# Filter taps and filter spectra joined into one block, with the filter network's vectors loaded as columns

## What is computed

```python
mod = jax.nn.silu(c) @ ada_w[l] + ada_b[l]          # the same for c_ctx
h = jnp.sin(fr * (z @ w1 + b1))
h = jnp.sin(fr * (h @ w2 + b2))
h = jnp.sin(fr * (h @ w3 + b3)) @ w4                # the taps, (L, 1024)
h = h * jnp.concatenate([decay, decay], axis=-1)
k = jnp.concatenate([hf, zeros, hb[:0:-1]], axis=0)
k = k / jnp.sum(jnp.abs(k), axis=0, keepdims=True)
y = irfft(rfft(v) * rfft(k))                        # rfft(k) is what the spectra are for
```

## Time and profile before

| | |
|---|---|
| median of three runs | 1666.65 us (1663.92 to 1668.58) |
| the profiled execution, its time | 1668.4 us |
| its span in the trace | 1666.5 us |
| instructions | 22924 |
| busy share of the span: PE, DVE, ACT, POOL | 94%, 59%, 29%, 29% |
| first block ends, second starts | about 90 us |
| second block ends, third starts | about 136 us |

### The profile page before, as it was taken

How to read it: one execution, slowest core, us unless ns; L and a number is a source line. 1 busy time by engine, 2 the same in 40 slices (tenths; PEclk the granted TensorE clock), 3 DMA queues, 4 the chain that set the end, 5 groups by cost and what they waited for, 6 DMA issues and landing times.

```text
span 1666.5 us, 22924 instructions
## 1 busy us (share of the span) xinstructions
PE 1565.5 (94%) x9583; PEld 1438.0 (86%) x9583; DVE 991.2 (59%) x1370; ACT 491.2 (29%) x694; POOL 485.9 (29%) x218
## 2 busy tenths in 40 slices
PE   4797999999989979899999999999999999999996
PEld 1386789988989969799889999999999999999995
DVE  5547233776534336813788827864884687288845
ACT  1565122232243237543522211310320221122203
POOL 1557121323121139225422322321331322232210
PEclk9889999999989989999999999999999999999998
DMA  8563313344343687520011101101101101101102
GB/s 338 185 253 152 158 40 121 129 165 148 109 157 123 231 257 255 172 92 26 4 48 51 51 29 48 51 28 50 51 26 51 51 26 51 51 26 51 51 13 114
DMA packets 110569, 168.10 MB, mean 101 GB/s; under 512 B 5755, under 2 KB 87811, under 8 KB 105347
## 3 DMA queue, kind: packets, MB, share of 16 engines
q1 hardware_dynamic: 109039, 164.24, 28.4%
q10 hardware_dynamic: 1428, 2.40, 0.5%
HBM read 135.35 MB, written 31.27 MB: 100 GB/s over the span
## 4 chain that ended last, share of the span: by engine, by line
PE 55%; DVE 3%; ACT 1%; issue 0%; POOL 0%; ACTq 0%; DVEq 0%
PE psum L231 18%; PE psum L233 18%; PE psum L235 18%; DVE mlp_acc_a L3056 1%; DVE tail_scan_h L2936 1%; PE psum L3160 0%; PE psum L3320 0%; DVE mlp_h_lo L2942 0%; DVE w_raw L3125 0%; DVE mlp_h_lo L2930 0%; DVE mlp_acc_a L3125 0%; DVE tail_x L3080 0%; DVE mlp_h_lo L2987 0%; ACT tail_x L2833 0%; PE psum L3191 0%
## 5 line engine op out<-in xcount | busy, mean ns | idle before, releaser
L231 PE MATMUL psum<-mlp_h_hi,w_hi 128*128 128x384 f32 (+2 forms) x1248 | 304.5, 339 | 6.2 <-DVE mlp_acc_a L3056 3.5
L233 PE MATMUL psum<-mlp_h_lo,w_hi 128*128 128x384 f32 (+2 forms) x1248 | 301.0, 336 | 0.0
L235 PE MATMUL psum<-mlp_h_hi,w_lo 128*128 128x384 f32 (+2 forms) x1248 | 300.8, 336 | 0.0
L3056 DVE SCALAR_TENSOR_TENSOR w_raw<-psum,par,w_raw 128x945 f32<-128x945 f32 (+2 forms) x176 | 214.7, 1220 | 90.7 <-ACT w_raw L2877 87.0
L3056 DVE SCALAR_TENSOR_TENSOR mlp_acc_a<-psum,par,mlp_acc_a 128x945 f32<-128x945 f32 (+2 forms) x176 | 214.5, 1219 | 33.1 <-ACT mlp_acc_a L2877 29.9
L2648 POOL TENSOR_TENSOR w_lo<-w_raw,w_hi 128x2048 fp32r<-128x2048 f32 x32 | 148.1, 4628 | 288.4 <-ACT w_hi L2642 288.4
L231 PEld LDWEIGHTS psum<-mlp_h_hi,w_hi 128*128 128x128 f32 x1248 | 205.0, 189 | 25.4 <-issue 6.3
L233 PEld LDWEIGHTS psum<-mlp_h_lo,w_hi 128*128 128x128 f32 x1248 | 206.2, 189 | 15.2
L235 PEld LDWEIGHTS psum<-mlp_h_hi,w_lo 128*128 128x128 f32 x1248 | 206.0, 189 | 15.3
L3080 DVE SCALAR_TENSOR_TENSOR tail_x<-psum,mod,tail_x 128x384 f32<-128x384 f32 (+1 forms) x192 | 94.8, 515 | 128.3 <-PE psum L235 128.1
L233 PE MATMUL psum<-tail_g_lo,w_hi 128*128 128x384 f32 x480 | 160.3, 334 | 0.0
(11 more groups left out here) (372 smaller groups left out, 2524.3 us busy)
## 6 DMA issues: line engine op xcount, KB each, us to landing
w_raw<-ffn_w_up SPq DMA_DIRECT2D x22, 1024.0 KB, 5.0
filt_ada<-ada_w SPq DMA_DIRECT2D x16, 1024.0 KB, 8.6
w_raw<-w_in SPq DMA_DIRECT2D x13, 1024.0 KB, 5.5
w_raw<-ffn_w_down SPq DMA_DIRECT2D x11, 1024.0 KB, 5.0
scan_rows_spread<-scratch_scan_rows SPq DMA_DIRECT2D x18, 512.0 KB, 5.5
rownorm_ada<-ada_w SPq DMA_DIRECT2D x8, 1024.0 KB, 7.6
rownorm_x<-x_sample SPq DMA_DIRECT2D x8, 512.0 KB, 8.0
scratch_kt<-kt_spec SPq DMA_DIRECT2D x4, 1024.0 KB, 4.1
```

Source lines behind the costliest of these rows:

```text
L231: ins = nc.tensor.matmul(out, wh, x_hi(k, i), start=begin, stop=False)
L233: ins = nc.tensor.matmul(out, wh, x_lo(k, i), start=False, stop=False)
L235: ins = nc.tensor.matmul(out, wl, x_hi(k, i), start=False, stop=end)
L3056: ins = stt(out=out, in0=image(up_at)[:, r0 + dy:r1 + dy, c0 + dx:c1 + dx], scalar=weight(i, loc, t), in1=out, op0=ALU.mult, op1=ALU.add)
```

## The change

The two blocks become one, `filter_and_spectra`.

- The four vectors of the network come as columns (`vec`, eight DMAs of 64 elements each), no longer through `rows` and the transpose. PE's first two matmuls are those of the first layer.
- The first operation of the argument, bias and frequency, moves from DVE to ACT (`scale_product`, an Identity with a scale and a bias); DVE makes `shifts = bias * freq` once.
- SP loads the first layer's weights and the first part of `ada_w` ahead of the rest; `w4`, the rows and the cosine tables take other places in its list.
- The 16 parts are spread as 6 over the network's halves, 1 in each of the steps 1 to 6, 2 in step 7, and 2 behind the first group of the spectrum. The first group of the modulation is copied in step 3 and turned in step 4, the second after step 8.
- Groups 0, 1 and 2 of the spectrum stand before the closing sums of the taps; the prompt's spectrum comes after them. The PSUM banks of `pair(g)` are exchanged for that, and the squares, roots and scalings of the RMS norm move on by one group.
- The cosine tables are split in steps 4 and 5 instead of 6 and 7.

```diff
+def filter_and_spectra(nc, io, mem, dram, buffers, k_hi, k_lo, norm, stage, spec_out):
+    PARTS, RING = 2 * KD, FILTER_RING
+    TURN_AT = 4
     PIECE = FW // 2
+    STEPS4 = [(kt, half) for kt in range(2) for half in range(2)]
...
+        ring = WeightRing(nc, ph, mem, lambda u: (full, 1 + 6 * u if u else 4), ahead=2)
         ps, par = mem["psum"], mem["par"]
-        ADA_BANK = 6
...
-        conv += [(io["c"][0].rearrange("(b p) -> b p", p=P), 60, 8), (io["c_ctx"].rearrange("(b p) -> b p", p=P), 68, 8)]
...
-        filt = [(io[n], 76 + i) for i, n in enumerate(("hy_filt_b1", "hy_filt_b2", "hy_filt_b3", "hy_freq"))]
...
+        vectors = [io[n].rearrange("o p -> p o") for n in ("hy_filt_b1", "hy_filt_b2", "hy_filt_b3", "hy_freq")]
...
-        sizes = [2, 3, 3] + [1, 1, 2, 2, 2, 0, 0, 0] + [0]
+        sizes = [2, 2, 2] + [1, 1, 1, 1, 1, 1, 2, 2]
         part_at = [range(sum(sizes[:i]), sum(sizes[:i + 1])) for i in range(len(sizes))]
         assert sum(sizes) == PARTS
-        FORWARD_AT = (6, 7)
+        FORWARD_AT = (4, 5)
+        FORWARD_AFTER = 8
...
+        def pair(g):
+            first = (2, 0, 6, 4)[g % 4]
+            return ps[:, first:first + 2, :]
+        def sums_at(g):
+            return g + 1 if g < 3 else g + 2
...
-            sp.dma_start(mem["ident"][:], io["k_ident"]).then_inc(ident_in, 16)
+            def load_layer(src, i, n, sem):
+                for half in range(2):
+                    at_ = 64 * half
+                    sp.dma_start(wide[at_:at_ + n, i, at_:at_ + 64], src).then_inc(sem, 16)
             sp.dma_start(h[:], io["k_z"]).then_inc(mlp_in, 16)
             sp.wait_ge(wide_zero, 1)
-            for src, i, n in layer_w:
-                for half in range(2):
-                    at_ = 64 * half
-                    sp.dma_start(wide[at_:at_ + n, i, at_:at_ + 64], src).then_inc(mlp_in, 16)
+            load_layer(*layer_w[0], mlp_in)
...
                 if p == 0:
+                    sp.dma_start(mem["ident"][:], io["k_ident"]).then_inc(ident_in, 16)
+                    for layer in layer_w[1:]:
+                        load_layer(*layer, layers_in)
+                if p == 1:
                     for half in range(2):
                         sp.dma_start(w4[64 * half:64 * half + 64, :], io["hy_filt_w4"][0]).then_inc(w4_in, 16)
-                if p == PARTS - 3:
-                    sp.dma_start(forward_raw(0), io["k_prompt"]).then_inc(forward_in[0], 16)
-                    sp.dma_start(forward_raw(1), io["k_fwd"][0]).then_inc(forward_in[1], 16)
-                if p == 2:
+                if p == RING - 1:
                     sp.wait_ge(zeroed, 1)
                     for dst, src in loads:
                         sp.dma_start(dst, src).then_inc(rows_in, 16)
+                if p == FORWARD_AFTER:
+                    sp.dma_start(forward_raw(0), io["k_prompt"]).then_inc(forward_in[0], 16)
+                    sp.dma_start(forward_raw(1), io["k_fwd"][0]).then_inc(forward_in[1], 16)
+            sp.wait_ge(forward_lo, 3)
+            load_forward(sp, ring, io, 2)
+            sp.wait_ge(part_done, PARTS)
+            sp.wait_ge(par_t, 6)
+            for g in range(3):
+                norm.load(sp, g)
+            for u in range(2):
...
-                if j == FORWARD_AT[0] + 1:
+                if j == FORWARD_AT[0]:
                     split_forward_lo(nc.gpsimd, 0, slice(0, forward_width(0)))
-            split_forward_lo(nc.gpsimd, 1, slice(0, UNIT // 2))
+                if j == FORWARD_AT[1]:
+                    split_forward_lo(nc.gpsimd, 1, slice(0, UNIT // 2))
+            step = Chain(pool, pool_step)
+            ring.split_lo(pool, 2)
...
+            def ada_part(p):
+                g, k = p // KD, p % KD
+                pe.wait_ge(ada_in[p % RING], 16 * (p // RING + 1))
+                for side in range(SIDES):
+                    last = nc.tensor.matmul(ps[32 * side:32 * side + 2, ADA_BANK + g % 2, :], cond[:, k, :],
+                                            ada[:, p % RING, side * AW:(side + 1) * AW], start=(k == 0), stop=(k == KD - 1))
+                last.then_inc(part_done, 1)
...
+            pe.wait_ge(vec_in, 16 * 8)
+            pe.wait_ge(mlp_in, 16 * 3)
+            for i in range(2):
+                mlp_half(0, i)
             pe.wait_ge(ident_in, 16)
-            pe.wait_ge(rows1_in, 16 * n_rows1)
+            pe.wait_ge(rows1_in, 16 * len(conv))
             pe.wait_ge(zeroed, 1)
             turn_rows(1)
-            pe.wait_ge(mlp_in, 16 * n_mlp)
-            mlp_layer(0)
+            pe.wait_ge(layers_in, 16 * 4)
             pe.wait_ge(cond_ready, 1)
-            ada_parts(0)
-            for layer in range(1, 3):
-                mlp_layer(layer)
-                if layer == 2:
-                    pe.wait_ge(rows_in, 16 * n_rows)
-                    pe.wait_ge(par_c, 1)
-                    for i in (0, 2, 3, 4, 5):
-                        turn_rows(i)
-                ada_parts(layer)
+            for layer in range(3):
+                for i in range(2):
+                    if layer:
+                        mlp_half(layer, i)
+                    if layer == 2 and i == 1:
+                        pe.wait_ge(rows_in, 16 * n_rows)
+                        pe.wait_ge(par_c, 1)
+                        for r in (0, 2, 3, 4, 5):
+                            turn_rows(r)
+                    for p in part_at[layer][i:i + 1]:
+                        ada_part(p)
...
-                if j in TURN_AT:
-                    turn_group(TURN_AT.index(j))
+                if j == TURN_AT:
+                    turn_group(0)
                 if j >= 2:
                     sum_sizes(j - 2)
-                if j >= 1:
-                    ada_parts(2 + j)
+                if 1 <= j < NT - 1:
+                    for p in part_at[2 + j]:
+                        ada_part(p)
+            pe.wait_ge(tapped, 2 * NT - 2)
+            pe.wait_ge(k_lo_done, NT - 1)
+            pe.wait_ge(forward_lo, 3)
+            spectrum(0)
+            for p in part_at[1 + NT]:
+                ada_part(p)
             sum_sizes(NT - 2)
+            pe.wait_ge(tapped, 2 * NT)
+            spectrum(1)
             sum_sizes(NT - 1)
+            pe.wait_ge(group_copied, 2 * SIDES)
+            spectrum(2)
+            turn_group(1)
             pe.wait_ge(sums_copied, 2)
-            pe.wait_ge(mod_done, PARTS // KD)
             for c in range(CH):
-                last = nc.tensor.transpose(ps[:, MOD_BANK, c * P:(c + 1) * P], part_rows[:, 0, c * P:(c + 1) * P], mem["ident"][:])
+                last = nc.tensor.transpose(ps[:, SIZE_BANK, c * P:(c + 1) * P], part_rows[:, 0, c * P:(c + 1) * P], mem["ident"][:])
             last.then_inc(norm_turned, 1)
+            pe.wait_ge(k_lo_done, NT)
+            pe.wait_ge(read, 1)
+            prompt_spectrum()
+            pe.wait_ge(mod_done, 2)
+            pe.wait_ge(norm_read, 1)
+            for g in range(3, 12):
+                if g == 4:
+                    pe.wait_ge(prompt_read, 1)
+                spectrum(g)
...
+            for i, src in enumerate(vectors):
+                for half in range(2):
+                    act.dma_start(vec[64 * half:64 * half + 64, i:i + 1], src).then_inc(vec_in, 16)
             act.wait_ge(zeroed, 1)
-            first = [(rows[r:r + n, 1, :], src) for src, r, n in conv]
-            first += [(rows[r:r + 1, 1, at_:at_ + 64], src) for src, r in filt for at_ in (0, 64)]
-            for dst, src in first:
-                act.dma_start(dst, src).then_inc(rows1_in, 16)
+            for src, r, n in conv:
+                act.dma_start(rows[r:r + n, 1, :], src).then_inc(rows1_in, 16)
...
+            def scale_product(layer, i):
+                act.wait_ge(mm, 2 * layer + i + 1)
+                nc.scalar.activation(arg[:, i * PIECE:(i + 1) * PIECE], ps[:, i, 0:PIECE], ACT.Identity, scale=vec[:, 3:4],
+                                     bias=shifts[:, layer:layer + 1]).then_inc(scaled, 1)
+            act.wait_ge(shifts_done, 1)
+            for i in range(2):
+                scale_product(0, i)
...
+                    if layer < 2:
+                        act.wait_ge(sin_done, 2 * layer + i + 1)
+                        scale_product(layer + 1, i)
...
-                if j + 1 in TURN_AT:
-                    copy_group(TURN_AT.index(j + 1))
+                if j == TURN_AT - 1:
+                    copy_group(0)
...
+            copy_group(1)
+            for g in range(12):
+                n = g // 3
+                if g == 2:
+                    copy_sums()
+                act.wait_ge(full, sums_at(g))
+                if n >= 2 and g % 3 == 0:
+                    act.wait_ge(spec_done, n - 1)
+                if n and g % 3 == 2:
+                    act.wait_ge(read, g - 2)
+                nc.scalar.activation(low_part(g).rearrange("p a c -> p (a c)"), pair(g)[:, 1, :], ACT.Copy).then_inc(odd, 1)
+                if g == 2:
```

(36 more changed lines are left out.)

308 lines of the change are left out of this document (124 added, 184 removed).

## The result

The changed kernel takes 1653.9 us, median of four executions (1653.27 to 1656.02), beside 1667.62 for the kernel before (four, 1663.92 to 1670.86): ratio 0.9924, interval 0.9906 to 0.9942, by the ratio 12.7 us less (the two medians lie 13.7 apart; against the 1666.65 on which the forecast was built it is 12.75). The forecast was 1650.4 with a range of 1642.5 to 1660.5: right in sign, inside the range, and 3.5 us too hopeful. The profiled execution took 1654.14 us (span 1652.0), where that of before took 1668.4 (span 1666.5).

What follows compares the result with a forecast made beforehand. It took DVE to bound the network, a chain over four engines the taps, and the drain to idle PE. Terms -4.5 - 5.5 - 8.5 + 2.2 = -16.3 us took the median from 1666.65 to 1650.4, range 1642.5 to 1660.5.

Steps and rivals of the forecast that it cites:

- A: The network, up to the first product of the taps: 4.5 us less; bounds 0 to 6.5.
- B: The taps, from the first product to the end of the eighth residual: 5.5 us less, 34.0 for 39.5.
- C: The drain and the prompt, from the eighth residual to the end of the prompt's spectrum: 8.5 us less.
- D: ACT's work behind the prompt, up to the block's end: 2.2 us more; bounds 0 and 4.
- only the join pays: Rival, chance 0.18: parts hold up the network, steps stay as long as before; 9.2 us less in all, 1657.5.
- All goes well: Rival, chance 0.12: group 0 at full clock, taps at their bound, network 5 us less; about 1645.5 us.
- Nothing arrives: Rival, chance 0.05: something not moved, such as loads of `x` and `w_in`, holds the joined block's end; 1666 us.
- slower: Rival, chance 0.03: the vectors' columns arrive late and hold the whole block; at 32 us slower by 5, 1671.7.
- the terms' bounds: Best and worst cases of the four terms together, said to reach from a gain of about 24 us to about 6.

Runs made afterwards that it cites:

- e1: Changed kernel with the network's first operation (bias and frequency) back on DVE and ACT's six scalings taken out; ratio 0.9962 to the kernel before.
- f2: Changed kernel with the network's four vectors loaded as rows and transposed again, ACT's scaling and the join kept; ratio 0.9934 to the kernel before.
- e5: Changed kernel with the four loads of the condition rows issued on SP's queue instead of ACT's; ratio 0.9935 to the kernel before.
- e2: Changed kernel with a one-element Silu ahead of ACT's first wait, so one early table load serves the network; ratio 0.9937 to the kernel before.
- e8: Changed kernel with both the early single table load and the condition rows' loads on SP's queue; ratio 0.9930 to the kernel before.
- e6: Changed kernel with the modulation parts of steps 5 to 7 moved behind group 0, six parts there instead of two; ratio 1.0012 to the kernel before.
- f1: Changed kernel with DVE's half of the cosine table's split one step later, behind the taps of step 7; ratio 0.9932 to the kernel before.
- e4: Changed kernel with POOL's residual of the third weight unit taken ahead of its wait for group 8; ratio 0.9930 to the kernel before.
- e3: Changed kernel with the last two modulation parts and both closing sums of the taps ahead of group 0; ratio 0.9956 to the kernel before.
- e9: Changed kernel with early single table load, condition rows' loads on SP's queue and POOL's early residual of the third weight unit; ratio 0.9918 to the kernel before.
- f4: Changed kernel with the edits of e9 plus DVE's half of the table split one step later; ratio 0.9921 to the kernel before.

## Why the prediction was right or wrong

**Right: what bounds the kernel, and that the join pays.** All engines meet at the end of the block, and what it wins there stays won: block 12.5 us earlier in the two profiles, total 12.7 by the ratio (10.0 when the kernel was measured again). It is luck in part that the time lies so well inside the range: A and B gave 5.6 us less than forecast, and C and D 1.8 us back, of which C's 0.6 by two errors that offset each other.

**A, mis-sized: -1.9 for -4.5** (-1.2 in the second profile). Its second half held (the operation off DVE: 3.0 forecast, 3.6 less from first range operation to first product, 3.9 shown by e1). The step that failed is "That will not come earlier: the transpose waits for the twelfth DMA of ACT's list, and the twelfth it remains". It remained the twelfth, but the place in a list is no time. ACT issues the six bias columns in 3.79 us in the kernel after (0.63 each) and the same six as rows in 2.17 in f2 (0.36 each). The list's last load is issued by 8.50 in the kernel after (7.84, 0.66 long) and by 6.97 in f2: that is 1.5 of the 3.2 us. The other 1.7 lie between this issue and the transpose, 6.4 us in the kernel after and 4.8 in f2. PE stood ready from 12.99 on, where the first layer's matmuls end, and waited 1.95 us more (the row names no releaser; in e5, with the rows issued sooner, there is no such wait). Why the rows take longer to land behind columns no run shows. So I counted DMAs and should have costed their issue and their landing.

What I built on that step failed too: that the first product is "already there and scaled" at 12.5. PE's matmuls start with the columns at 10.49, and the first half is scaled at 13.9; with the table loaded early (e2) at 12.9. So no run brings DVE's first range operation back to the 13.97 of before: it starts at 15.28 in f2, where the rows are early and the products late, and at 14.45 in e8. That the load ahead of the Silu costs nothing was right: it ran from 14.44 to 15.72, and the Silu started right behind the copied rows. The other load, ahead of the first scaling, I had not priced. It was covered only because the rows were late; with early rows it costs 0.5 us (14.96 in e5, 14.45 in e8). That the parts cause no stall of PE beyond 2 us in the network was right.

**B, mis-sized: -2.5 for -5.5.** "POOL waits some 1.4 us once, and is full afterwards" is the step that failed. POOL waited 1.90, 1.95, 0.60 and 0.51 us in steps 2 to 5, and with two short waits at the end 5.4 in all, where I had 3.0 (1.4 and eight handovers of 0.2). The first of these waits came behind the decay's load. For the others PE needs 3.54 us for a step: the product 1.7, the sums and a part 1.8; in step 3 ACT's copy of a group (2.41 us, until 54.46) stood ahead of the high part for 0.6 us as well. I had priced the part (1.04) and not laid it end to end with the product and the sums; e6 shows that the pitch is the part's. Second, I took DVE's half of the split to run beside POOL's half. It does not: it starts at 65.74, POOL's ends at 68.07, and DVE's 1.09 us behind that (69.16); in f1 POOL's residual ends at 72.91 and DVE's split 1.08 us behind it (73.99). And POOL's next residual, started at 68.00, then takes 3.39 us for 2.40. The Trainium skill, page SBUF — State Buffer, section Who interferes with whom, says that the two engines share a port pair as an exclusive lock, which a DVE operation with two inputs in SBUF wants too, and that the loser blocks for the other's whole instruction. The trace agrees with it in all three places: of DVE's 3.42 us some 2.3 are waiting, and of POOL's 3.39 some 1.0.

B also has a scatter of its own. The same code took 36.7 to 37.1 us in both profiles of the changed kernel and in e1, e2, e4, e5 and e8, but 38.4 in e3 and 39.5 in e9 and f2. In f2 PE is granted 0.88 from 52 to 72 us, in the changed kernel 1.00: two of f2's matmuls still take 1.05 us at 53.11, where such a pair takes 0.62 at 2.4 GHz, and DVE waits 2.83 and 2.92 us before its taps of steps 3 and 4. f4 belongs to the late ones too (38.2, where f1 with the same split took 35.7). The windows of the kernel after and then of f2, each ahead of PE's pause before step 2 and behind it, show what these four have in common:

```profile
44.00:46.00 2.00, 1.81 (x5) 0.90 (x3) 1.12 (x2) 2.00 (x4) 1.76 (x1) 0.50 0.89 258
52.00:55.00 3.00, 3.00 (x15) 1.24 (x15) 1.98 (x3) 2.90 (x6) 1.67 (x1) 1.00 1.05 374
```

```profile
44.00:46.00 2.00, 1.15 (x5) 0.82 (x4) 1.12 (x3) 2.00 (x3) 1.25 (x1) 1.00 0.80 184
52.00:55.00 3.00, 3.00 (x14) 1.36 (x13) 0.80 (x2) 2.92 (x5) 2.19 (x1) 0.50 0.96 351
```

In e3, e9, f2 and f4 the clock had risen to 2.4 GHz once already, between 41 and 44 us. PE then stood still for 2.5 to 3.2 us, the clock fell in that pause or within 1.3 us behind it, and it came back only at 55 to 57. In the other profiles it stayed at 1.2 GHz through the pause and rose at 50 to 52 (54 in e1). Why it rose early in the four is open.

**C, right: -9.1 for -8.5, and by luck as near.** Group 0 started 0.11 us behind the eighth residual; parts, sums, transposes and prompt followed without a wait over 0.2. But two items of the sum were wrong and offset each other. I had given group 0 the low clock, 5.1 us; in the two profiles of the changed kernel it ran at 2.4 GHz (matmuls 0.12 us apart) and took 3.0. And I had one closing sum at 0.4; there are two, and each takes 0.95. The other items came out within 0.5 us each, and in sum within 0.2. In the other profiles in which group 0 stands first (e1, e2, e4, e5, e6, e8, e9, f1, f2, f4) the matmuls are 0.21 us apart from its start or from 0.7 us behind it on, and from group 0 to the end of the prompt it takes 16.6 us (16.5 in f4; e6 has its parts there). My term, 15.7 with the handover, lies between 15.1 and 16.6.

**D, half: +1.0 for +2.2.** The copy of group 8 stands 19.4 us behind the prompt, where I had 20.5 and before it was 18.3. ACT is busy for 17.1 of the 19.4 us. What I overpriced was this work, 19.0 us in my sum: the operations overlap by about 0.1 us each, so that a copy takes 0.5 of the list and not 0.6, and a square with its read 1.0 to 1.1 and not 1.25. The waits between were more than I had, 2.2 us (1.06 and 1.16) for 1.6. e4 shows that the +1.0 is not needed.

**The rivals.** That only the join pays (1657.5) is as near to the time (3.6 us) as my forecast (3.5), and the number does not decide between them; the marks do. C and D came about as in both, but B moved by 2.5 us where the rival has nothing. Its mechanism fell as well: PE never waits for `filt_ada` in the network of the kernel after, and DVE waits for the decay in one step. "All goes well" had the clock of group 0 right for the changed kernel, but fell with A and B. "Nothing arrives" and "slower" fell: the columns came at 10.5 us, and ACT did not stand for `rownorm_x`. One sum of the prediction does not come out: the terms' bounds reach from a gain of 24.3 us down to 1.6 (0 + 0 + 5.6 - 4), not to "about 6".

## What to carry to other kernels

Cost a list of loads by its issue rows and its landings, and not by its length in instructions: a load that keeps its number can still be issued 1.5 us later and arrive 3 us later when those ahead are cut into columns. When an edit puts small work on an engine between the steps of a chain, lay that engine's whole step end to end before you name the engine that bounds. And do not give half of an elementwise job to DVE beside the other half on GpSimd without a row that shows the two at once: here the sum of both was paid, POOL's next operation was held for 1.0 us, and both reached the chain.

## What the hardware showed that I had not expected

- DMA issue on ACT's queue: 0.63 us for a column of 64 elements, 0.29 to 0.36 for a row of 64.
- Three products of 320 columns on DVE take 1.54 us alone and 3.44 to 3.67 beside a GpSimd operation; they end 1.40 us behind GpSimd's (33.18 to 34.58 in the kernel after), as if they had hardly begun before.
- The clock of group 0, right behind nearly the same steps, was 2.4 GHz in the two profiles of the changed kernel and 1.2 for some 3 us in its ten variants that start with this group, which makes 1.5 us. Two of two against none of ten suggests that it goes with the code; no run settles it. Behind the blocks the rest of the kernel varied from 1526.0 to 1531.2 us. The same steps took 36.7 to 39.5 us, by when the clock rose. Gains under some 2 us in the head can vanish in that.
